# Replanning the first stage of a decoder trunk: samples' projection tiles first, cache pages at 4/3 steps per tile, retention states by heads, half of the output projection ahead of the samples

## The reference, cut to what matters

```python
proj = h @ w_in
rq, rk, rv, rg, dq, dk, dv = jnp.split(proj, EVEN_SPLITS, axis=-1)
ro, s_fin = retention(rq, rk, rv, s0)          # samples: S = gamma*S + k^T v; o = q S
ro = head_group_norm(ro) * jax.nn.silu(rg)
dq = rope(rms_norm(dq, qg), pos); dk = rope(rms_norm(dk, kg), pos)
k_all = concatenate([k_past, dk]); v_all = concatenate([v_past, dv])
do = diff_attn(dq, k_all, v_all, ...)          # (softmax(q1 k1) - lam softmax(q2 k2)) v
mix = concatenate([ro, do]) @ w_out
```

## Time and profile before

| | us |
|---|---|
| median of 3 runs | 2041.03 (2038.61 to 2042.01) |
| the profiled execution's own time | 2045.41 |
| its span, from the first to the last instruction | 2043.6 |
| TensorE busy in the span | 1882.8 |
| VectorE, GpSimd, ScalarE busy | 909.9, 636.0, 568.6 |

### The profile page before, as it was taken

The page is one execution under the profiler, slowest core; times in us unless marked ns, Lnnn a source line. Parts: engine busy times, 40 slices in busy tenths (PEclk is TensorE's granted clock), DMA queues, the critical chain, the costliest instruction groups (busy, mean ns, idle before and its releaser), DMA issues.

```text
span 2043.6 us, 35465 instructions
## 1 busy us (share of the span) xinstructions
PE 1882.8 (92%) x14237; PEld 1683.9 (82%) x14237; DVE 909.9 (45%) x1155; ACT 568.6 (28%) x915; POOL 636.0 (31%) x510
## 2 busy tenths in 40 slices
PE   4967888899998799999999999979999999999998
PEld 4855555555554599999999899879999999999997
DVE  2577676665552544332333423393323443323331
ACT  4422333322231232221222232303313333212221
POOL 1388554777740013300431100023304224102400
PEclk8988898999996799999999999979999999999999
DMA  6258686899997223332323322202322232332221
GB/s 206 92 165 270 232 258 207 315 335 356 337 320 243 94 83 94 99 92 90 92 93 93 95 63 82 67 10 74 101 86 92 89 98 83 104 91 86 92 93 63
DMA packets 218268, 287.95 MB, mean 141 GB/s; under 512 B 12977, under 2 KB 149762, under 8 KB 217858
## 3 DMA queue, kind: packets, MB, share of 16 engines
q1 hardware_dynamic: 215306, 281.95, 41.8%
q10 hardware_dynamic: 2208, 2.75, 0.4%
q0 software_dynamic: 624, 1.44, 0.4%
HBM read 274.89 MB, written 11.21 MB: 140 GB/s over the span
## 4 chain that ended last, share of the span: by engine, by line
PE 81%; DVE 8%; DMA 3%; ACT 3%; SPq 2%; issue 2%; POOL 1%; ACTq 0%; DVEq 0%
PE ps L1639 18%; PE ps L1641 18%; PE ps L1640 18%; PE ps L1449 6%; PE ps L1451 5%; PE ps L1450 5%; PE ps L1495 4%; DMA vbuf<-in_cache_v 2%; DVE Sc L1138 1%; PE ps L1540 1%; POOL kbuf L633 1%; PE ps L1706 1%; PE ps L1422 1%; PE ps L1527 1%; PE ps L1519 1%
## 5 line engine op out<-in xcount | busy, mean ns | idle before, releaser
L488 DVE TENSOR_TENSOR w_lo<-raw,w_hi 128x1024 fp32r<-128x1024 f32 x238 | 334.7, 1414 | 498.2 <-ACT w_hi L481 497.1
L1639 PE MATMUL ps<-xg_hi,w_hi 128*128 128x260 f32 x1408 | 398.6, 283 | 0.5 <-DVE sTs L1409 0.5
L1641 PE MATMUL ps<-xg_hi,w_lo 128*128 128x260 f32 x1408 | 398.4, 283 | 0.0
L1640 PE MATMUL ps<-xg_lo,w_hi 128*128 128x260 f32 x1408 | 397.3, 282 | 0.0
L633 POOL TENSOR_TENSOR kbuf<-kbuf,Qb 128x512 f32<-128x512 f32 x256 | 344.4, 1373 | 141.0 <-DMA kbuf<-in_cache_k 140.9
L481 ACT ACTIVATE w_hi<-raw 128x1024 fp32r<-128x1024 f32 x248 | 259.1, 1054 | 460.9 <-PE ps L1641 413.0
L1449 PE MATMUL ps<-w_hi,xg_hi 128*128 128x256 f32 (+1 forms) x1200 | 352.4, 294 | 21.8 <-DVE w_lo L488 9.4
L1450 PE MATMUL ps<-w_lo,xg_hi 128*128 128x256 f32 (+1 forms) x1200 | 344.6, 287 | 0.0
L1451 PE MATMUL ps<-w_hi,xg_lo 128*128 128x256 f32 (+1 forms) x1200 | 344.2, 287 | 0.0
L1641 PE MATMUL ps<-h_hi,w_lo 128*128 128x260 f32 x1024 | 289.3, 283 | 0.0
L1639 PE MATMUL ps<-h_hi,w_hi 128*128 128x260 f32 x1024 | 289.1, 282 | 0.0
(11 more groups left out here) (274 smaller groups left out, 2543.0 us busy)
## 6 DMA issues: line engine op xcount, KB each, us to landing
kbuf<-in_cache_k SPq DMA_DIRECT2D x256, 256.0 KB, 4.5
vbuf<-in_cache_v SPq DMA_DIRECT2D x256, 256.0 KB, 4.9
raw<-in_w_ffn_up SPq DMA_DIRECT2D x64, 512.0 KB, 3.8
raw<-in_w_ffn_down SPq DMA_DIRECT2D x64, 512.0 KB, 3.5
raw<-in_w_in_odd SPq DMA_DIRECT2D x48, 512.0 KB, 3.8
raw<-in_w_in_even SPq DMA_DIRECT2D x36, 512.0 KB, 5.5
raw<-in_w_out_odd SPq DMA_DIRECT2D x24, 512.0 KB, 3.6
raw<-in_w_out_even SPq DMA_DIRECT2D x12, 512.0 KB, 3.6
```

Of the source, the lines that this page charges most:

```text
L488: dve.tensor_tensor(w_lo[:, c.slot], raw[:, c.slot % 2], w_hi[:, c.slot].bitcast(F32), ALU.subtract).then_inc(lo_made, 1)
L1639: pe.matmul(out, wh, xh, start=kk == 0, stop=False, skip_group_check=True)
L1640: pe.matmul(out, wh, xl, start=False, stop=False, skip_group_check=True)
L1641: mm_ = pe.matmul(out, wl, xh, start=False, stop=kk == KC * groups - 1, skip_group_check=True)
```

## The change

- **The order of the tiles.** `TILES` begins with the samples' tiles of macros 0 and 1, which are the samples' queries; from macro 2 on the samples' tile stands first in its macro. The prologue scales and splits the 8 sample columns by themselves, ahead of the prompt, and loads chunks 2 and 3 into a buffer of their own, `early`. The samples' queries and keys get a rotation of their own (`ropeS`, 8 partitions, two macros in one step); the prompt's `rope` works on 4 tiles and not on 5.
- **The pace of the cache steps.** They start at tile 4 and come at 4/3 per tile. The values are 22 steps behind the keys, and `STEPS` is 153. Counted from the two plans:

| tiles through | key pages before, after | value pages before, after |
|---|---|---|
| 30 | 40, 68 | 0, 24 |
| 56 | 144, 138 | 104, 96 |
| 90 | 256, 228 | 240, 184 |

- **The units** of the prompt's attention stand at every 1.5 tiles from tile 30 and not at every tile.
- **`lo` of the first chunks** is on DVE; before, ten of them were on POOL (`LO_SWITCH` is gone).
- **The states by heads.** `sL` loads the states of one head in four transfers of two samples, `sM` masks the keys, four `sU` make the outer product and the update, `sO` reads and stores. They stand between the tiles from tile 59 on, 8 tiles a head, in buffers of their own.
- **The mixed rows** lie over `xg_hi` and `xg_lo` (`ma`) and beside them (`mb`), so their transposes (`mix`) stand among the cache steps behind the last tile. The later layers' split input gets a place of its own (`xb`).
- **`prompt_first`**: the first macro of the output projection multiplies its first 260 columns before it waits for the samples' columns.

The core of the diff:

```diff
-LAG = SPS + 4
+LAG = SPS + 6
-LO_SWITCH = 5
+FIRST_STEP = 4
+def _tiles():
+    seq = [(0, NT), (1, NT)]
+    for m in range(N_IN):
+        seq += [(m, NT)] * (m > 1) + [(m, t) for t in range(NT)]
+    return seq
...
     for m in ROPED:
-        after[m + 1, 0].append(("rope" if m < 4 else "rot", m))
-        after[m + 2, 0].append(("turn", m, 0))
-        after[m + 2, 1].append(("turn", m, 1))
+        first[read_of(m)].append(("rope" if m < 4 else "rot", m))
+        for hh in range(2):
+            first[read_of(m) + 5 + hh].append(("turn", m, hh))
+    for i in range(len(UNITS)):
+        j = AT[6, NT] + 3 * i // 2
+        middle[j].append(("dA", i))
+        first[j + 1].append(("dE", i))
+        first[j + 2].insert(0, ("dT", i))
+        late[j + 2].append(("dB", i))
...
+        j = AT[12, NT] + 8 * h
+        first[j - 1].append(("sL", h))
+        first[j - 1].append(("sM", h))
+        for p in range(NS // 2):
+            first[j + p].append(("sU", h, p))
+        first[j + NS // 2].append(("sO", h))
...
-    for m in range(3, N_IN):
-        for t in range(NT + 1):
-            for n in range(2):
-                if step < STEPS and (n == 0 or m > 4):
+    for j in range(slots):
+        n = max(0, (j - FIRST_STEP + 1) * 4 // 3) - step if j < NTILE else 2
...
-            pool.wait_ge(lo_made, AHEAD)
-                    if m < LO_SWITCH and t == 1:
-                        lo(pool, Chunk(0, 0, 0, 2 * m + AHEAD))
...
-                    for s in range(NS):
-                        sp.dma_start(s0b[:, s], state_ret[0, s].rearrange("h d e -> d h e")).then_inc(s0_loaded[s], 16)
+                        for p in range(NS // 2):
+                            sp.dma_start(s0[p][:, :, :], state_ret[0, 2 * p:2 * p + 2, h].rearrange("s d e -> d s e")
+                                         ).then_inc(s0_loaded[p], 16)
...
-            wide("oe", 4, mT_hi, mT_lo, mix_lo, [14, 14, 14])
+            wide("oe", 4, mixed(ma_hi, mb_hi), mixed(ma_lo, mb_lo), mix_lo, [13, 13, 13], begin=prompt_first)
```

More of the change, by code:

```diff
@@ L14 @@
+import itertools
 import math
@@ L1608, in _ @@
[L1608 to L1618 removed]
+            for j, now in enumerate(AFTER):
+                if j < NTILE:
+                    m, t = TILES[j]
+                    if j == 0:
+                        pe.wait_ge(xs_made, 1)
+                    if j == AT[0, 0]:
+                        pe.wait_ge(xg_lo_made, KD)
+                    if t == NT:
+                        pe.wait_ge(lo_made, 2 * m + 2)
+                    wait(pe, nat_read, j - 1)
+                    natural([Chunk(0, 0, 0, 2 * m + g) for g in range(2)], t, NAT[j % 2], xg_hi, xg_lo, NT - 1)
+                for step in now:
+                    pe_step(step)
@@ L1620, in wide @@
+            def wide(name, per, high, low, ready, counts, e=None, first=1, begin=None):
                 c0, groups, macros = PHASES[name]
```

731 lines of the change are left out of this document (410 added, 321 removed).

## The result

The changed kernel takes 2067.62 us (median of 4 runs, 2059.36 to 2071.62), the kernel before in the same session 2041.52 (4 runs, 2038.61 to 2045.26). The ratio is 1.0123, with a 95% interval of 1.0094 to 1.0151. I had forecast 1987, a range of 1937 to 2022, and 0.06 for slower. The profiled execution took 2066.42 us with a span of 2064.5.

A forecast was written before the change was run, and what follows sets the result against it. VectorE's rotations were taken to hold stage A, no full engine B, transfers C, serial work the tail. +15 - 40 - 25 - 4 = -54 us gave 1987 us as a median, range 1937 to 2022.

The forecast's parts named there:

- Stage C: Tiles 57 to 90, 219.9 us before, taken as bound by transfers; with fewer pages 195 us, 25 won.
- stage A: First 30 tiles, held by VectorE; 123.6 us of work plus waits, ending at 185, 15 us later than before.
- the tail: From tile 90 to the output projection; remaining pages at 333 GB/s, 76 us for 79.4, 4 won.
- The 11: In stage C, us added because two limits of the same size get in each other's way in ordered queues.
- Rival 3: Stage C's tiles come no faster, since `sU` holds VectorE until states land; C 220, total 2012 or 2027; chance 0.15.
- Rival 4: In the tail, value pages come one quad per round trip, 8.2 us each; 38 us slower, 2079; chance 0.06.
- the 20 for waits: In stage A, us added to VectorE's 123.6 us of work for its waits.
- the lower one: Stage A's lower bound, an end at 155, if every rotation costs its price alone and there are no waits.
- The 9.95 us: In stage A, the price of one VectorE rotation without GpSimd beside it; 14.8 us while GpSimd weighs pages.
- The rule that I had weighed: In stage A, VectorE and GpSimd exclude each other by a lock; 141 us, stage end at 182 at the earliest.
- Stage B: Tiles 31 to 56, no engine full; fewer pages and half the exponent waits gone, 232 becomes 192, 40 won.
- The rest: From the output projection on 1342 us as before; the prologue unchanged at about 41.1, within 3 us.

The follow-up runs named there:

- g1: Changed kernel with two cache steps per tile from tile 56 on, but one at tile 56 itself; 2038.56 us, ratio 0.997.
- e3: Changed kernel without the samples' retention states (no loads, products, updates, reads or stores of them); 2033.28 us, ratio 0.9956.
- f1: Changed kernel with a unit of attention at every tile again, not at every 1.5 tiles; 2081.53 us, ratio 1.0184.
- f2: Changed kernel with the cache-step pace of the kernel before and a unit of attention at every tile; 2043.35 us, ratio 1.0008.
- f3: Changed kernel without page loads behind the first eight of each cache; 1981.36 us, ratio 0.97.
- h1: Kernel before the change without page loads behind the first eight of each cache; 1985.57 us, ratio 0.9718.
- h2: Changed kernel without page loads behind the first eight of each cache and without the samples' states; 1936.7 us, ratio 0.9479.
- e1: Changed kernel with only the pace of the cache steps as in the kernel before; 2054.16 us, ratio 1.0055.

## Why the prediction was wrong, step by step

**Stage C, "195, 25 won": the step that failed.** It was 239.5, 44.5 more, of the 74 us by which the stages together missed. It is the largest miss and not the only one: with C alone right the sum would still have said 9.5 us faster; stage A (17.3 more) or the tail (15.0 more) has to be right as well before the sign is. By the runs, against the 219.9 of before: 70 pages fewer at 0.41 us (g1) is 29 less; the states 28.5 more (e3); the norms 12.6 to 15.1 more (f1, f2); left over 5 to 8. The terms come from different kernels, so this sum is an estimate. Three things in the forecast were wrong.

- I took the lower bound of C to be two loads of equal size, 182 for transfers and 184 for TensorE, and added 11 for their meeting. TensorE's sum was not far off in what it counted: in f3 it is busy 199.4 us. But the stage takes 219.8 in f3 without any page to wait for, and loads then add 19.7. The 11 stands for what measured 220 - 184 + 20 = 55. The profile of before showed it: TensorE idle 14 us of 220, at a clock of 0.98, beside transfers at 0.94; I read this as bound by transfers, and h1 says that without them C would still have been 192.7.
- I priced the states at 30 us on TensorE, which is right (33), and then let them vanish under transfers. They don't: taken out, they give back 28.5 us with page loads (e3) and 39.2 without (h2).
- The norms of the attention are in no term. They were in B before, in slots 48 to 51, and the wider spacing of the units pushes them to slots 56 to 59, which is C. There VectorE's first instruction of them waits 11.1 us for ScalarE. A step that is moved by another edit's arithmetic has to be looked for; they stand in the plan, not in the diff.

Rival 3 (C stays at 220, at 0.15) named the right place. Its mechanism, VectorE held by late states, is not there (6.2 us once), and C came out 20 us longer still. The way to a slower kernel through C was not among my rivals; the one that I gave for slower went through the tail.

**The tail, "76".** 91.0, 15.0 more. Rival 4 (one quad per round trip, 8.2 us) did not come: 60 value pages took 60.8 us from 662.8 to 723.6, 4.05 us per quad. That is the 4.1 of two overlapping round trips, which I had named as the reason against rival 4, "18 us more at most", and then left out of the sum, where a quad has 3.1. Here is the chain near its end, in order of time:

```profile
701.59 3.68 DMA vbuf<-in_cache_v
705.31 3.33 PE ps L1587 x8
708.65 0.31 SPq L544
...
710.16 3.96 DMA vbuf<-in_cache_v
714.16 1.69 PE ps L1587 x4
715.87 0.30 SPq L544
...
717.89 5.63 DMA vbuf<-in_cache_v
723.56 1.04 PE ps L1587 x2
```

Each product of a quad is followed by SyncE's wait for it, the issue, and 4 to 6 us of landing. I had 333 GB/s and 24.4 MB, with 3.1 MB taken off for pages that were to lie in the buffers already. Measured are 300 GB/s over 26.4 MB up to 724: both factors were some 10 per cent off. The DMA share is 0.89 there, so the runs don't tell how much of the 15 us is the round trip and how much the rate. The first product on `ma_hi` starts at 726.69, with no gap behind the first 72, so that `prompt_first` does what it says.

**Stage A, "+15".** +32.5. The sum of VectorE's work, 123.6, was high: it is busy 109.65 (68 key sums 43.3 against 43.9, splits 13.8 against 16.3, four rotations 36.2 against 47.4, the samples' 13.9 against 11.0). The step that failed is the 20 for waits, which were 51.5. f3 has 137.7 for the stage where I had 143.9, and loads add 23.5; that the forecast comes within 6 us of f3 is in part luck, since its work was too high and its waits too low there too (VectorE idles 27.7 us in f3). Of the bounds, the lower one is wrong by its own terms: 123.6 with 32 for the rotations and no waits gives 149, not 155.

The rotations were misread. The 9.95 us that I took as the price without GpSimd has a split of GpSimd's in it, and the instruction beside that split takes three and a half times as long as its twin behind it:

```profile
74.20 2.70 POOL L488 TENSOR_TENSOR w_lo<-raw,w_hi 128x1024 fp32r<-128x1024 f32 x1 [4.38 <-ACT w_hi L481]
74.68 2.90 DVE L1079 TENSOR_TENSOR swp<-stg,gain_sin 128x640 f32<-128x640 f32 x1
77.50 0.81 DVE L1080 TENSOR_TENSOR swp<-stg,gain_sin 128x640 f32<-128x640 f32 x1
```

And not all four rotations of the changed kernel meet a GpSimd that weighs pages. These are their stretches, GpSimd's busy time behind the length:

```profile
64.60:73.70 9.10, 3.13 (x2) 1.00 0.30 98
85.80:98.30 12.50, 12.50 (x8) 0.67 0.34 119
120.60:127.50 6.90, 0.00 (x0) 0.56 0.00 0
149.30:158.30 9.00, 2.98 (x2) 1.00 0.42 137
```

A rotation of 128x1024 takes 6.9 us alone and 12.5 us beside GpSimd's products. Here are rows of the second rotation, with GpSimd's products, and of the third:

```profile
85.14 14.29 POOL L685 TENSOR_TENSOR kbuf<-kbuf,Qb 128x512 f32<-128x512 f32 x8 [1.11 <-DMA kbuf<-in_cache_k]
85.80 1.21 DVE L1154 TENSOR_REDUCE tiny<-swp 128x16 f32<-128x1024 f32 x1
92.71 2.19 DVE L1163 TENSOR_TENSOR stg<-stg,gain_cos 128x1024 f32<-128x1024 f32 x1
120.63 1.20 DVE L1154 TENSOR_REDUCE tiny<-swp 128x16 f32<-128x1024 f32 x1
124.98 1.23 DVE L1163 TENSOR_TENSOR stg<-stg,gain_cos 128x1024 f32<-128x1024 f32 x1
```

The reduction keeps its time, and each of the six two-input instructions takes 0.5 to 1.1 us longer. GpSimd pays too: its eight products take 1.79 us each, and 1.28 in the median where no two-input instruction overlaps them. The rule that I had weighed (the Trainium skill, SBUF — State Buffer, section "Who interferes with whom") is an exclusive lock between these two, and the trace agrees with it in kind. It does not show that the two never overlap: the six instructions take 10.7 us, where their 5.2 alone and the about six products beside them at 1.28 would make 12.9, an estimate from these rows. The rule's sum of 141 us also has two terms that are not those of the main sum: rotations at 32 and splits at 16 make it 136, an end at 177 and not 182. Either way the real end, 200.7, is behind it, and the rows say why: GpSimd waits for keys.

```profile
POOL kbuf L685 <- DMA kbuf<-in_cache_k: 55.4, 16, 12.2
```

**Stage B, "192".** 195.6, and that is luck. I gave 29.8 us to the fewer pages and 10.2 to the spacing of the units; f1 shows 32.3 for the spacing with the norms and, against the 232.0 of before, 4 for all the rest. By the estimate above, 12.6 to 15.1 of the 32.3 are the norms, which were not saved but moved to C, and 17 to 20 the spacing. The waits for the exponent alone fell by 11.8 (20.4 to 8.6), close to the 10.2. The pages' transfers are worth 4.4 there (f3).

**The rest** was as forecast: 1337.7 us where the kernel before has 1339.6 from the same event on; and the prologue within 3.

What stays open is the part of C's 54 us in e1 beyond states (28.5 to 33.0) and norms (12.6 to 15.1), some 6 to 13 us; new places of the softmax steps and their lag of two more are candidates, and were not tried apart.

## What to carry to other kernels

Take the transfers away before you call a stage bound by them: a stage with a DMA share of 0.94 kept 88 per cent of its time without page loads, and most of the work that was moved into it was paid in full. Where one in-order queue loads for several consumers, ask for each load which wait stands ahead of it: here one line that puts value pages first was worth 17 to 23 us, and nothing in the kernel before. When a plan's spacing is changed, list what else the new slots push across a stage's border; a stage that lost it looks faster than it is. And before a row serves as a price "without" another engine, look at what that engine did in it.

## What the runs showed of the hardware

- TensorE's granted clock was lower where TensorE waited more. In stage B it is 0.93 on average with the wide spacing, where TensorE is busy 0.87 of the stage, and 0.84 with the narrow one (f1), where it is busy 0.82. A product of a prompt tile by `w_hi` and `xg_hi` took 297 ns on average at 0.98 (stage C of before) and 339 at 0.80 (stage B of f2). So what is waited for in another engine is in part paid a second time.
- A page of 256 KB landed in a median of 4.5 us in stage C of e3, at 262 GB/s, and of 5.2 in that of the kernel before, at 333. So the lower rate came from fewer transfers in flight, and not from slower ones.
- VectorE's two-input instructions and GpSimd's products lengthened each other (12.5 us for a rotation in place of 6.9, 1.79 us for a product in place of 1.28); reductions on VectorE did not grow (1.21 and 1.20 us).
